# Expert loop of a two-block model: rows gathered already turned, biases in four row groups, four units of weights held, loads moved ahead

## The chip, the cores and the metric

The kernel runs on one core of a Trainium2 chip. The metric is the device time of one execution in microseconds; less is better. Three runs of the kernel before gave 2664.05, 2665.75 and 2666.48 us (median 2665.75). The profile is of one more execution.

## What is computed

A sequence of 256 tokens of width 1024 passes through two blocks, all in float32. The first block is two layers of a hybrid of convolution, retention and window attention. The second block is one layer: a token mixer with a bidirectional recurrence over 256 context and 256 latent tokens, and then a mixture of 32 experts of which each token takes 4. The change is in the last part and in what is loaded just ahead of it. Its reference, in short:

```
logits = h @ w_router + b_router                 # (256, 32)
top_val, top_idx = top_k(logits, 4); gates = softmax(top_val)
for each expert e, for the tokens that chose it:
    u   = h[tok] @ w1[e] + b1[e]                 # (n, 2048)
    glu = min(u[:, 0::2], 7); lin = clip(u[:, 1::2], -7, 7)
    act = glu * sigmoid(1.702 * glu) * (lin + 1)
    out[tok] += gate * (act @ w2[e] + b2[e])     # (n, 1024)
x = layer_norm(alpha * x + gt2 * out)
```

An expert has 8 MiB of w1 (1024 x 2048) and 4 MiB of w2 (1024 x 1024).

## The kernel before, in words

Each engine has its own program, and semaphores order them. The experts are done in jobs: one job is one expert with at most 64 of its tokens (SLOTS). There are 32 jobs, and one more for each further 64 tokens of an expert that has more; the count is computed on the chip (`turns`), and in the profiled execution it is 33. `moe_tensor`, `moe_scalar` and `moe_vector` each have a loop over the jobs; `moe_loads` is the loop of SyncE, which starts the transfers.

The weights of a job are six units of 2 MiB: units 0 to 3 are w1, units 4 and 5 are w2. There are six slots for them (`slots`: three of the ring that the whole kernel uses, and three of `ring2`). The load of unit j of job t+1 is started when TensorE has used unit j of job t (`e_unit`). Job 16 (`KEPT`) is special: its units 4 and 5 are loaded ahead of the loop into buffers of their own (`extra`), and in the loop only its units 0 to 3 are loaded.

TensorE does in a job, in this order (lines 2578 to 2631):

1. The biases of w1 for the job's expert: four products of a 32 x 64 selector with 32 x 512 of b1 (L2592), into banks 4 and 5. They all lie on partitions 0 to 31; two of them write the lower and two the upper 64 partitions of a bank.
2. The up projection: 32 products of 128 x 64 by 128 x 512 (L2601), stationary `hsel`, moving the weights.
3. The gather for the next job: four products with the stationary selector `sel` (128 x 64) and the moving tokens `h_tok` (128 x 512), into bank 6 (L2549).
4. The scatter of the job before: eight products of 64 x 128 by 64 x 256 into banks 0 to 3 (L2563), which hold the sums over all jobs.
5. Two transposes of the gated selector (L2614), four of the gathered rows (L2555, `turn_gathered`) and four of the job's hidden rows (L2621). The gathered and the hidden rows are read with a step of four elements (`[:, c::4]`).
6. The down projection: 16 products of 128 x 64 by 128 x 512 (L2629).

A float32 product is two pairs of LDWEIGHTS and MATMUL in the trace, a transpose is one. ScalarE copies between these steps: `gsel` (L2685, gathered rows out of bank 6), `selgT` (L2708), `hsel` (L2688), `hidT` (L2712) and `ye` (L2715), and computes the two sigmoids (L2703). VectorE makes the selectors and the gated product.

Ahead of the loop TensorE does the gather of job 0, starts the sums in banks 0 to 3 with b2 (L2539: eight products of 32 x 128 by 32 x 256, all on partitions 0 to 31, in two calls of `start_sums`), and turns the gathered rows between the two calls. SyncE starts job 0's unit 1 after the last weights of the token mixer, waits for the end of the mixer's output projection (`mo_done` 4), and then starts unit 2, unit 0, `grids`, `b2`, `b1`, units 3, 4, 5 and job 16's units 4 and 5.

Of the kernel before, what the change touches and what calls it, by code (L numbers as in the profile page):

```python
# [1332 lines left out]
def mixer_tensor(pe, nc, g):  # L1333
# [318 lines left out]
    for n in range(4):  # L1652
        pe.wait_ge(g["gn_squared"].sem, g["gn_squared"].at(None, n + 1))
        nc.tensor.matmul(flat[4 + n], blk64, g["squares"][:, n, :], start=True, stop=True).then_inc(
            g["gn_sum"].sem, g["gn_sum"].one())
# [43 lines left out]
def mixer_scalar(act, nc, g):  # L1699
# [188 lines left out]
    for n in range(4):  # L1888
        act.wait_ge(g["gn_sum"].sem, g["gn_sum"].at(None, n + 1))
        nc.scalar.activation(g["squares"][:, n, :], flat[n], ACT.Square).then_inc(g["gn_squared"].sem, g["gn_squared"].one())  # L1890
    for n in range(4):
        act.wait_ge(g["gn_sum"].sem, g["gn_sum"].at(None, 5 + n))
        nc.scalar.activation(g["squares"][:, n, :], flat[4 + n], ACT.Ln, bias=g["eps2"][:, 1:2], scale=1.0 / C2).then_inc(
            g["gn_log"].sem, g["gn_log"].one())
    act.wait_ge(g["gn_log"].sem, g["gn_log"].at(None, 4))
    for n in GN_ORDER:
        nc.scalar.activation(g["squares"][:, n, :], g["squares"][:, n, :], ACT.Exp, scale=-0.5).then_inc(
            g["gn_root"].sem, g["gn_root"].one())
# [12 lines left out]
def mixer_aliases(g):  # L1911

    g["norms"] = [g["squares"][:, NC:DN, 0:T], g["yy"][:, 0:NC, :]]
    g["cat"] = g["stack"][:, :, 0:T]

    g["incl"] = [g["squares"][:, 0:NC, :], g["stack"][:, NC:DN, :]]
    g["excl"] = [g["stack"][:, 0:NC, :], g["squares"][:, NC:DN, :]]
    g["gate"] = g["stack"][:, :, T:2 * T]
    g["bonus_in"] = g["m_k"].rearrange("p n (s t) -> p (n s) t", s=2)
    g["bonus"] = g["kd"][:, :, 0:T]  # L1920
    g["fa"] = g["iclr"][:, :, 0:T]
    g["spec"] = g["kk"][:, :, 0:T]
# [402 lines left out]
EXTRA = 16  # L2325
JOBS = N_EXPERTS + EXTRA
# [19 lines left out]
def moe_grids():  # L2346
# [3 lines left out]
    return np.concatenate([grids, np.arange(P)[:, None]], axis=1).astype(np.float32)  # L2350


def moe_signals(ctx, nc, g, hyb):
# [5 lines left out]
    for name, spent, base, per in (  # L2359
        ("u_first", "x_sum", 0, 1), ("ga_done", "conv_sum", 1, 1), ("gb_done", "ret_scores", 1, 1), ("st_done", "ret_o", 1, 1),  # L2360
        ("ht_done", "ret_var", 0, 1), ("ga_out", "x_root", 1, 1), ("st_out", "conv_root", 1, 1), ("ht_out", "decay_ready", 0, 1),
# [11 lines left out]
    g["extra_in"] = [follow(g["start_in"], g["start_in"].per, 1), Signal(ctx, nc, "extra_in", 1, 16)]  # L2373


def moe_memory(ctx, nc, g):
# [8 lines left out]
    sb("b2", [D], parts=N_EXPERTS)  # L2385
    sb("b1", [2 * D_FF], parts=N_EXPERTS)
    sb("grids", [2 * GRID + 1])
    sb("h3", [DC, T])
# [17 lines left out]
    sb("gT", [T], parts=N_EXPERTS)  # L2406
    sb("sel", [TC, SLOTS])
    sb("selg", [TC, 2, SLOTS])
    sb("bsel", [SLOTS])
    sb("selgT", [T])  # L2410
    sb("gsel", [4 * P])
    sb("hsel", [4, 2, SLOTS])
    sb("glu", [2, 2 * P])
    sb("lin", [2, 2 * P])
    sb("sig", [2, 2 * P])
    sb("hid", [4 * P])
    sb("hidT", [4, 2, SLOTS])
    sb("ye", [4 * P])
    sb("finrow", [2, T])
    sb("tiles", [T])  # L2420
    extra = sb("extra", [2, DC * UNIT])
    g["extra"] = {4: extra[:, 0], 5: extra[:, 1]}
    g["fin"] = g["h3"]

# [7 lines left out]
def moe_loads(sp, nc, g):  # L2432
    def unit(e, j, slot):

        if j < 4:
            rows = g["w1"][0, bass.ds(e, 1), (j // 2) * 4 * P:(j // 2 + 1) * 4 * P, :]
            src = rows.rearrange("o (p c) n -> p (o c) n", c=4)[:, 2 * (j % 2):2 * (j % 2) + 2, :]
            return sp.dma_start(slot.rearrange("p (c n) -> p c n", c=2), src)
        rows = g["w2"][0, bass.ds(e, 1), (j - 4) * 4 * P:(j - 3) * 4 * P, :]
        return sp.dma_start(slot.rearrange("p (c n) -> p c n", c=4), rows.rearrange("o (p c) n -> p (o c) n", c=4))  # L2440
# [12 lines left out]
    for j, s in zip((4, 5), g["extra_in"]):  # L2453
        unit(KEPT, j, g["extra"][j]).then_inc(s.sem, s.one())
# [3 lines left out]
    def job(t, units):  # L2458
        e = KEPT if type(t) is int else sp.value_load(g["jobs"][0:1, bass.ds(t, 1)], min_val=0, max_val=N_EXPERTS - 1)
        for j in units:  # L2460

            sp.wait_ge(g["e_unit"].sem, t * E_UNITS + (j + 1))
            unit(e, j, g["slots"][j]).then_inc(landed(j).sem, landed(j).unit)
# [3 lines left out]
    job(KEPT, range(4))  # L2467
# [19 lines left out]
MOE_LOOP = ("e_unit", "u_first", "ga_done", "st_done", "gb_done", "ht_done")  # L2487


def moe_tensor(pe, nc, g):  # L2490
# [87 lines left out]
    def job(t, kept=0):  # L2578
        def landed(j):
            if type(t) is int and j in g["extra"]:  # L2580
                s = g["extra_in"][j - 4]
                pe.wait_ge(s.sem, s.at(None, 1))
# [33 lines left out]
        pe.wait_ge(g["ga_out"].sem, g["ga_out"].at(t, 1))  # L2616
        turn_gathered().then_inc(g["gb_done"].sem, g["gb_done"].one())
# [41 lines left out]
def moe_scalar(act, nc, g):  # L2659
# [9 lines left out]
    nc.scalar.activation(g["finrow"][0:1, 0, 0:1], g["eps3"][0:1, 0:1], ACT.Exp)  # L2669
# [11 lines left out]
    nc.scalar.activation(g["gT"][:, :], flat[7][0:N_EXPERTS, 0:T], ACT.Copy).then_inc(  # L2681
        g["gates_out"].sem, g["gates_out"].one())

    def take_gathered():
        return nc.scalar.activation(g["gsel"][:, :], flat[6], ACT.Copy)  # L2685
# [5 lines left out]
    take_gathered().then_inc(g["ga_out"].sem, 1)  # L2691
    act.wait_ge(g["gb_done"].sem, g["gb_done"].at(None, 0))
# [7 lines left out]
    with act.Fori(0, turns) as t:  # L2700
# [16 lines left out]
    nc.scalar.activation(g["finrow"][0:1, 0, 0:1], g["eps3"][0:1, 0:1], ACT.Copy).then_inc(g["all_out"].sem, 1)  # L2717
    nc.scalar.activation(g["finrow"][0:1, 1, 0:1], g["eps3"][0:1, 0:1], ACT.Sqrt)
# [14 lines left out]
def moe_vector(dve, nc, g):  # L2733
# [77 lines left out]
    v.tensor_copy(g["bhot"][:, 0:N_EXPERTS], g["c"]("ident")[:, 0:N_EXPERTS])  # L2811
# [13 lines left out]
    dve.wait_ge(g["late_in"].sem, g["late_in"].at(None, 3))  # L2825
# [91 lines left out]
def program(nc, w, out):  # L2917
    with ExitStack() as ctx:
# [44 lines left out]
        moe["late_in"] = Signal(ctx, nc, "late_in", 3, 16)  # L2963
# [9 lines left out]
        def _(sp):  # L2973
# [7 lines left out]
            moe_loads(sp, nc, moe)  # L2981
# [86 lines left out]
```

## Time and profile before

| | us |
|---|---|
| median of three runs | 2665.75 (2664.05 to 2666.48) |
| profiled execution, its own time | 2661.23 |
| its span | 2658.4 |
| mean granted TensorE clock | 0.994 of full |
| TensorE busy | 2544.8 (96%) |
| VectorE busy | 924.9 (35%) |
| ScalarE busy | 583.4 (22%) |
| moved by DMA | 636.13 MB, mean 239 GB/s |

The span runs from the first instruction to the last; 2.8 us of the execution's time lie around it. PE is TensorE's matmul, PEld its weight load, and the two overlap. DVE is VectorE, ACT ScalarE, POOL GpSimd and SP SyncE. The jobs fill the span from about 1689 us to 2639 us.

### The profile page before, as it was taken

How to read it: one execution, taken by the hardware profiler on the slowest of the kernel's cores; microseconds unless marked ns; L12 is line 12 of the kernel's file. 1: busy time of each engine (PE TensorE's matmuls, PEld its weight loads, DVE VectorE, ACT ScalarE, POOL GpSimd, SP SyncE). 2: the span in 40 equal slices, each digit the busy share in tenths (PEclk: the TensorE clock that was granted, in tenths of full speed). 3: DMA queues.
4: the chain of work that ended last, by engine and by line, in shares of the span. 5: the costliest groups of instructions: out<-in, count | busy, mean ns of one | idle time of the engine just before them, and what ended most of it. 6: DMA issues, size and time to landing. Idle time of an engine off the chain costs nothing.

```text
span 2658.4 us, 42182 instructions
## 1 busy us (share of the span) xinstructions
PE 2544.8 (96%) x18014; PEld 1673.4 (63%) x18014; DVE 924.9 (35%) x2004; ACT 583.4 (22%) x1168; POOL 149.5 (6%) x124
## 2 busy tenths in 40 slices
PE   8999999999999999999997889899999999999998
PEld 6867878888884887888886777433333333333333
DVE  1863363312277245323476653311111111111112
ACT  2100233301100123220135433311111111111112
POOL 0050000000032000000003220000000000000000
PEclk9999999999999999999999999999999999999999
DMA  7555232344455422336410002999999999999995
GB/s 262 198 182 198 100 122 98 124 158 159 175 204 176 173 95 96 127 128 214 162 64 4 4 4 108 420 428 428 428 428 429 428 428 427 429 428 428 429 427 251
DMA packets 135029, 636.13 MB, mean 239 GB/s; under 512 B 5120, under 2 KB 5392, under 8 KB 109136
## 3 DMA queue, kind: packets, MB, share of 16 engines
q1 hardware_dynamic: 133904, 629.78, 59.6%
q0 software_dynamic: 992, 4.37, 0.5%
q8 instruction: 109, 1.79, 0.3%
q14 instruction: 24, 0.20, 0.0%
HBM read 633.08 MB, written 1.05 MB: 239 GB/s over the span
## 4 chain that ended last, share of the span: by engine, by line
PE 94%; ACT 2%; DVE 2%; issue 1%; DMA 1%; SPq 0%; ACTq 0%; DVEq 0%
PE bank L268 26%; PE bank L2601 17%; PE bank L2629 9%; PE bank L459 6%; PE bank L1405 4%; PE bank L481 4%; PE bank L289 4%; PE bank L1356 4%; PE bank L2563 2%; PE bank L2592 2%; PE bank L2549 2%; PE bank L1664 1%; PE bank L357 1%; PE bank L2621 1%; ACT hidT L2712 1%
## 5 line engine op out<-in xcount | busy, mean ns | idle before, releaser
L268 PE MATMUL bank<-hT,ring 128*128 128x256 f32 x3136 | 689.8, 380 | 2.5 <-DMA ring<-in_w_in 1.4
L268 PEld LDWEIGHTS bank<-hT,ring 128*128 128x128 f32 x3136 | 592.8, 190 | 94.6 <-issue 13.3
L2601 PE MATMUL bank<-ring,hsel 128*64 128x512 f32 x2112 | 462.0, 595 | 0.0
L2601 PEld LDWEIGHTS bank<-ring,hsel 128*64 128x64 f32 x2112 | 149.0, 137 | 310.8 <-issue 310.5
L2874 DVE TENSOR_SCALAR glu<-bank 128x256 f32<-128x256 f32 x66 | 28.0, 425 | 754.2 <-PE bank L2601 750.9
L2629 PE MATMUL bank<-ring,hidT 128*64 128x512 f32 x1024 | 226.8, 595 | 22.0 <-ACT hidT L2712 22.0
L754 DVE SCALAR_TENSOR_TENSOR a_buf<-v_pad,par,a_buf 128x256 f32<-128x256 f32 x480 | 215.8, 529 | 0.0
L2629 PEld LDWEIGHTS bank<-ring,hidT 128*64 128x64 f32 x1024 | 70.5, 137 | 156.2 <-issue 128.1
L1405 PE MATMUL bank<-ring 64*64 64x64 f32 (+1 forms) x5696 | 133.3, 229 | 25.6 <-issue 9.3
L1405 PEld LDWEIGHTS bank<-ring 64*64 64x64 f32 x5696 | 120.9, 137 | 40.6 <-issue 12.1
L2703 ACT ACTIVATE sig<-glu 128x256 f32<-128x256 f32 x66 | 27.5, 417 | 458.8 <-DVE glu L2874 458.8
L289 PE MATMUL bank<-ring,hT 128*128 128x512 f32 x256 | 111.4, 594 | 0.0
L481 PE MATMUL bank<-ro,ring 128*128 128x256 f32 x512 | 111.4, 379 | 0.0
L481 PEld LDWEIGHTS bank<-ro,ring 128*128 128x128 f32 x512 | 97.0, 190 | 13.8 <-issue 0.8
L1356 PE MATMUL bank<-stack,ring 128*128 128x256 f32 x480 | 104.5, 379 | 0.0
L1356 PEld LDWEIGHTS bank<-stack,ring 128*128 128x128 f32 x480 | 91.1, 190 | 12.7 <-issue 0.3
L289 PEld LDWEIGHTS bank<-ring,hT 128*128 128x128 f32 x256 | 48.2, 190 | 60.0 <-issue 60.0
L1232 POOL TENSOR_TENSOR ring<-ring,mcons 128x256 f32<-128x256 f32 x80 | 62.4, 815 | 250.9 <-DVE ring L2173 250.9
L2715 ACT ACTIVATE ye<-bank 128x512 f32<-128x512 f32 x33 | 19.7, 597 | 237.2 <-PE bank L2629 237.2
L2563 PEld LDWEIGHTS bank<-selgT,ye 64*128 64x128 f32 x544 | 49.7, 186 | 33.0 <-issue 26.8
L2563 PE MATMUL bank<-selgT,ye 64*128 64x256 f32 x544 | 67.9, 389 | 0.8 <-ACT finrow L2717 0.8
L2549 PE MATMUL bank<-h_tok,sel 128*64 128x512 f32 x272 | 64.2, 592 | 0.5 <-DVE sel L2796 0.5
(435 smaller groups left out, 2467.6 us busy)
## 6 DMA issues: line engine op xcount, KB each, us to landing
ring<-in_w SPq DMA_DIRECT2D x196, 2048.0 KB, 16.7
ring<-in_w_in SPq DMA_DIRECT2D x66, 2048.0 KB, 7.8
ring<-in_w_ada SPq DMA_DIRECT2D x12, 2048.0 KB, 8.0
ring<-in_w_ret_out SPq DMA_DIRECT2D x8, 2048.0 KB, 7.8
ring<-in_w_out SPq DMA_DIRECT2D x6, 2048.0 KB, 8.6
ring<-in_w_conv_out SPq DMA_DIRECT2D x4, 2048.0 KB, 8.3
ring<-in_w_attn_out SPq DMA_DIRECT2D x4, 2048.0 KB, 8.0
extra<-in_w SPq DMA_DIRECT2D x2, 2048.0 KB, 34.7
```

Source lines behind the costliest of these rows:

```text
L268: mm = nc.tensor.matmul(out[:, j, :], w[:, k, col + j * P:col + (j + 1) * P], rhs[:, k, :], start=(k == 0), stop=(k == DC - 1))
L289: mm = nc.tensor.matmul(out[:, :, :].rearrange("p a b -> p (a b)"), g["hT"][:, k, t * P:(t + 1) * P], w[:, k, :], start=(k == 0), stop=(k ...
L459: mm = nc.tensor.matmul(out[:, j, :], ws[k // DC][:, k % DC, cols + j * P:cols + (j + 1) * P], rhs[:, k, :], start=(k == 0), stop=(k == n ...
L481: mm = nc.tensor.matmul(out[:, j, :], w[:, k, col:col + P], g["ro"][:, row * DC + k, :], start=(row == 0 and j == 0 and k == 0), stop=(row ...
L754: ins = nc.vector.scalar_tensor_tensor(out=y[:, c, :], in0=v[:, c, t:t + T], scalar=w, in1=y[:, c, :], op0=ALU.mult, op1=ALU.add)
L1232: nc.gpsimd.tensor_tensor(g["cut"][:, k, d * NC:(d + 1) * NC, :], g["MP"][:, d * NC:(d + 1) * NC, :], row(mask[:, k, d, :], NC), ALU.mult) ...
L1356: mm = nc.tensor.matmul(flat[(q + 3) % 4][:, 0:T], w[:, k, j * P:(j + 1) * P], g["stack"][:, k, lo:lo + T], start=(k == 0), stop=(k == DC ...
L1405: mm = nc.tensor.matmul(out[at:at + 64], lhsT[lo:lo + 64], rhs[lo:lo + 64], start=start, stop=stop, skip_group_check=not (start and stop))
L2549: mm = nc.tensor.matmul(half(flat[6], side), g["sel"][:, t, :], g["h_tok"][:, t, side * UNIT:(side + 1) * UNIT], start=(t == 0), stop=(t = ...
L2563: mm = nc.tensor.matmul(g["bank"][b][:, at, :], half(g["ye"], side)[:, n * P:(n + 1) * P], half(g["selgT"], side), start=False, stop=last, ...
L2601: mm = nc.tensor.matmul(half(flat[4 + b], side), g["hsel"][:, 2 * (j % 2) + k, j // 2, :], w[:, at:at + UNIT], start=False, stop=(j == 3 a ...
L2629: mm = nc.tensor.matmul(half(flat[7], side), g["hidT"][:, c, j, :], w[:, at:at + UNIT], start=(j == 0 and c == 0), stop=(j == 1 and c == 3))
```

## The change

What it does:

- **Gather.** The operands change places: `h_tok` (128 x 128, read with a step of four elements) is stationary and `sel` (128 x 64) moves. The result lands in bank 6 in the layout of `hsel`, and one copy of ScalarE takes it there. The turning of gathered rows (`turn_gathered`, `take_gathered`, `gsel`, the semaphores `ga_out` and `gb_done`) goes.
- **Biases.** b1 and b2 lie in four groups of 32 partitions, each with a quarter of the columns, loaded by eight transfers in place of two. The selector and the gates (`bsel`, `gT`) stand four times over, once in each group; the gates are turned by eight products in place of two transposes. Each of the four bias products, and each of the eight of `start_sums`, takes the partitions of its group.
- **Buffers.** `h3`, the three grids of the overflow plan, and `glu`, `lin`, `sig`, `hid` share one buffer; `hidT` and `finrow` lie over `grids`; the mixer's group norm uses `m_k` in place of `squares`. The room goes to two more held units: job 16's units 2 to 5 are held, and the loop loads its units 0 and 1.
- **Loads.** Job 0's and the held units start in another order, and most of them earlier: four behind the mixer's last weights, one when the mixer's rows are done (`cat_ready` 2), one when half of its output projection is done (`mo_done` 2).

The diff, cut to its core:

```diff
@@ moe_memory
-    g["extra"] = {4: extra[:, 0], 5: extra[:, 1]}
+    g["extra"] = {2: extra[:, 0], 3: extra[:, 1], 4: extra[:, 2], 5: extra[:, 3]}
+    g["h3"] = shared[:, :].rearrange("p (c t) -> p c t", c=DC)
+    for i, name in enumerate(("before", "onehot", "work")):
+        g[name] = shared[:, i * GRID:(i + 1) * GRID].rearrange("p (o e) -> p o e", o=EXTRA)
+    for i, name in enumerate(("glu", "lin", "sig", "hid")):
+        g[name] = shared[:, i * 4 * P:(i + 1) * 4 * P]
...
@@ moe_loads
-    for j in (1, 2, 0):
-        if j == 2:
-            sp.wait_ge(g["mo_done"].sem, g["mo_done"].at(None, 4))
-        unit(0, j, g["slots"][j]).then_inc(landed(j).sem, landed(j).unit)
-    for dst, what in (("grids", g["grids_dram"]), ("b2", g["b2_dram"][0]), ("b1", g["b1_dram"][0])):
-        sp.dma_start(g[dst][:, :], what).then_inc(g["late_in"].sem, g["late_in"].one())
-    for j in (3, 4, 5):
-        unit(0, j, g["slots"][j]).then_inc(landed(j).sem, landed(j).unit)
-    for j, s in zip((4, 5), g["extra_in"]):
-        unit(KEPT, j, g["extra"][j]).then_inc(s.sem, s.one())
+    first(1)
+    kept(4)
+    first(4)
+    kept(3)
+    sp.wait_ge(mixer["cat_ready"].sem, mixer["cat_ready"].at(None, 2))
+    kept(5)
+    sp.wait_ge(g["mo_done"].sem, g["mo_done"].at(None, 2))
+    first(2)
+    sp.wait_ge(g["mo_done"].sem, g["mo_done"].at(None, 4))
+    first(0)
+    sp.dma_start(g["grids"][:, :], g["grids_dram"]).then_inc(g["late_in"].sem, g["late_in"].one())
+    for name, width in (("b2", D // GROUPS), ("b1", 2 * D_FF // GROUPS)):
+        for q in range(GROUPS):
+            sp.dma_start(g[name][q * N_EXPERTS:(q + 1) * N_EXPERTS, :],
+                         g[name + "_dram"][0, :, q * width:(q + 1) * width]).then_inc(g["late_in"].sem, g["late_in"].one())
+    first(3)
+    first(5)
+    sp.wait_ge(g["x_part"].sem, g["x_part"].at(None, DC))
+    kept(2)
...
-    job(KEPT, range(4))
+    job(KEPT, range(2))
@@ moe_tensor
-        mm = nc.tensor.transpose(flat[7][0:N_EXPERTS, t * P:(t + 1) * P], g["gate_map"][:, t, 0:N_EXPERTS], ident)
+        for q in range(GROUPS):
+            mm = nc.tensor.matmul(flat[7][q * N_EXPERTS:(q + 1) * N_EXPERTS, t * P:(t + 1) * P], g["gate_map"][:, t, 0:N_EXPERTS],
+                                  ident, start=True, stop=True)
...
-        for n in range(first, first + 4):
-            nc.tensor.matmul(g["bank"][n // 2][:, n % 2, :], g["b2"][:, n * P:(n + 1) * P], g["gT"][:, :],
-                             start=(n % 2 == 0), stop=False, skip_group_check=True)
+        for i in range(2):
+            for q in range(GROUPS):
+                lo, hi = q * N_EXPERTS, (q + 1) * N_EXPERTS
+                nc.tensor.matmul(g["bank"][q][:, i, :], g["b2"][lo:hi, i * P:(i + 1) * P], g["gT"][lo:hi, :],
+                                 start=(i == 0), stop=False, skip_group_check=True)
...
     def gather():
-        for t in range(TC):
-            for side in range(2):
-                mm = nc.tensor.matmul(half(flat[6], side), g["sel"][:, t, :], g["h_tok"][:, t, side * UNIT:(side + 1) * UNIT],
-                                      start=(t == 0), stop=(t == 1))
-        return mm
-
-    def turn_gathered():
         for c in range(4):
-            mm = nc.tensor.transpose(flat[6][:, c * P:(c + 1) * P], g["gsel"][:, c::4], ident)
+            for j in range(2):
+                for t in range(TC):
+                    mm = nc.tensor.matmul(flat[6][:, (2 * c + j) * SLOTS:(2 * c + j + 1) * SLOTS],
+                                          g["h_tok"][:, t, j * UNIT:(j + 1) * UNIT][:, c::4], g["sel"][:, t, :],
+                                          start=(t == 0), stop=(t == 1))
         return mm
...
+    pe.wait_ge(g["turned_out"].sem, g["turned_out"].at(None, 2))
     gather().then_inc(g["ga_done"].sem, 1)
-    start_sums(0)
-    pe.wait_ge(g["ga_out"].sem, g["ga_out"].at(None, 0))
-    turn_gathered().then_inc(g["gb_done"].sem, 1)
-    start_sums(4)
+    start_sums()
...
-                at = (2 * side + b) * UNIT
-                nc.tensor.matmul(half(flat[4 + b], side), g["bsel"][0:N_EXPERTS, :], g["b1"][:, at:at + UNIT], start=True, stop=False)
+                lo, hi = (2 * side + b) * N_EXPERTS, (2 * side + b + 1) * N_EXPERTS
+                nc.tensor.matmul(half(flat[4 + b], side), g["bsel"][lo:hi, :], g["b1"][lo:hi, :], start=True, stop=False)
...
-        pe.wait_ge(g["ga_out"].sem, g["ga_out"].at(t, 1))
-        turn_gathered().then_inc(g["gb_done"].sem, g["gb_done"].one())
@@ moe_scalar, in the loop
         act.wait_ge(g["ga_done"].sem, g["ga_done"].at(t, 1))
-        take_gathered().then_inc(g["ga_out"].sem, g["ga_out"].one())
+        take_rows().then_inc(g["gt_out"].sem, g["gt_out"].one())
         act.wait_ge(g["st_done"].sem, g["st_done"].at(t, 1))
         nc.scalar.activation(g["selgT"][:, :], flat[7][:, 0:T], ACT.Copy).then_inc(g["st_out"].sem, g["st_out"].one())
-        act.wait_ge(g["gb_done"].sem, g["gb_done"].at(t, 1))
-        take_rows().then_inc(g["gt_out"].sem, g["gt_out"].one())
@@ mixer: group norm
-        nc.scalar.activation(g["squares"][:, n, :], flat[n], ACT.Square).then_inc(g["gn_squared"].sem, g["gn_squared"].one())
+        nc.scalar.activation(g["gn_sq"][:, n, :], flat[n], ACT.Square).then_inc(g["gn_squared"].sem, g["gn_squared"].one())
...
```

## Rows read from the trace of the kernel before

**Rows 1.** The page: the chain that ended last, by engine.

```profile
PE 94%; ACT 2%; DVE 2%; issue 1%; DMA 1%; SPq 0%; ACTq 0%; DVEq 0%
```

**Rows 2.** The chain in order of time, one job and the next: start, us, what.

```profile
1733.58 1.72 PE bank L2549 x8
...
1739.50 7.09 PE bank L2629 x32
1746.59 1.86 PE bank L2592 x8
1748.45 13.88 PE bank L2601 x64
1762.33 1.72 PE bank L2549 x8
```

**Rows 3.** A stretch of the loop: length, busy of PE, PEld, DVE, ACT, POOL, clock, DMA, GB/s.

```profile
1704.23:2604.00 899.77, 877.79 (x4326) 329.70 (x4324) 126.69 (x384) 154.58 (x254) 0.00 (x0) 1.00 1.01 428
```

**Rows 4.** Landing of units 4 and 5 early; then of units 0 to 3, last job.

```profile
DMA to landing us min/median/max: 9.8/10.5/11.2
...
L2438 SPq DMA_DIRECT2D ring<-in_w x4: 332/332/342, 2586.2 to 2596.5; - x4
...
DMA to landing us min/median/max: 19.9/22.1/24.3
```

**Rows 5.** Timeline inside one job: start, us, engine, line, operation, shapes, idle before.

```profile
1704.65 1.88 PE L2549 MATMUL bank<-h_tok,sel 128*64 128x512 f32 x8
...
1706.47 2.00 PE L2563 MATMUL bank<-selgT,ye 64*128 64x256 f32 x16
...
1708.87 0.38 ACT L2708 ACTIVATE selgT<-bank 128x256 f32<-128x256 f32 x1 [1.69 <-PE bank L2614]
...
1709.30 0.56 PEld L2621 LDWEIGHTS bank<-shared_cons,hid 128*128 128x128 f32 x4 [0.18 <-ACT selgT L2708]
...
1710.09 0.60 ACT L2712 ACTIVATE hidT<-bank 128x512 f32<-128x512 f32 x1
```

**Rows 6.** Loads of 128 columns with little to move: timeline, then min/median/max in ns.

```profile
1679.00 0.39 PE L2523 MATMUL bank<-chosen_map,moec 128*128 128x32 f32 x2
1679.22 0.61 PE L2525 MATMUL bank<-chosen_map,shared_cons 128*128 128x32 f32 x4
...
1708.39 0.20 PEld L2614 LDWEIGHTS bank<-shared_cons,selg 128*128 128x128 f32 x2 [0.33 <-issue]
1708.56 0.56 PEld L2555 LDWEIGHTS bank<-shared_cons,gsel 128*128 128x128 f32 x4
...
L2614 PEld LDWEIGHTS bank<-shared_cons,selg x66: 138/140/143, 1708.4 to 2628.7; 128*128 128x128 f32 x66
L2555 PEld LDWEIGHTS bank<-shared_cons,gsel x136: 195/210/218, 1684.8 to 2629.1; 128*128 128x128 f32 x136
```

**Rows 7.** Lines by form: products that share the array in four tiles.

```profile
L232 PE MATMUL bank<-ring,cond 128*32 128x512 f32 x192 | 23.1, 598 | 0.0
L1405 PE MATMUL bank<-ring 64*64 64x64 f32 x5184 | 118.3, 223 | 25.2 <-issue 9.3 <-ACT ring L1833 5.1 <-DVE ring L2231 5.0
```

**Rows 8.** Timeline ahead of the loop; the last row is job 0's up projection.

```profile
1680.97 1.94 PE L2549 MATMUL bank<-h_tok,sel 128*64 128x512 f32 x8 [0.51 <-DVE sel L2796]
1682.84 1.99 PE L2539 MATMUL bank<-gT,b 32*128 32x256 f32 x8
...
1689.36 15.46 PE L2601 MATMUL bank<-ring,hsel 128*64 128x512 f32 x64
```

**Rows 9.** SyncE's issues; two stretches (columns as rows 3); landing of the held units.

```profile
1621.89 37.29 SPq L2438 DMA_DIRECT2D ring<-in_w  x3
...
1694.71 10.62 SPq L2438 DMA_DIRECT2D ring<-in_w  x4
...
1645.00:1650.00 5.00, 5.00 (x25) 4.40 (x24) 1.14 (x3) 0.00 (x0) 0.00 (x0) 1.00 0.00 0
1690.00:1695.00 5.00, 5.00 (x20) 1.56 (x18) 2.88 (x8) 0.61 (x1) 0.00 (x0) 0.76 0.99 419
...
extra<-in_w SPq DMA_DIRECT2D x2, 2048.0 KB, 34.7
```

More of the change, by code:

```diff
@@ L1653, in mixer_tensor @@
         pe.wait_ge(g["gn_squared"].sem, g["gn_squared"].at(None, n + 1))
-        nc.tensor.matmul(flat[4 + n], blk64, g["squares"][:, n, :], start=True, stop=True).then_inc(
+        nc.tensor.matmul(flat[4 + n], blk64, g["gn_sq"][:, n, :], start=True, stop=True).then_inc(
             g["gn_sum"].sem, g["gn_sum"].one())
@@ L2325 @@
 EXTRA = 16
+GROUPS = P // N_EXPERTS
 JOBS = N_EXPERTS + EXTRA
@@ L2349, in moe_grids @@
     grids = np.broadcast_to(np.concatenate([o.reshape(-1), e.reshape(-1)]), (P, 2 * GRID))
-    return np.concatenate([grids, np.arange(P)[:, None]], axis=1).astype(np.float32)
+    return np.concatenate([grids, np.arange(P)[:, None] % N_EXPERTS], axis=1).astype(np.float32)
 def moe_signals(ctx, nc, g, hyb):
@@ L2372, in moe_signals @@
         g[name] = follow(hyb[spent], DEPTH * hyb[spent].per + base, per)
-    g["extra_in"] = [follow(g["start_in"], g["start_in"].per, 1), Signal(ctx, nc, "extra_in", 1, 16)]
+    g["extra_in"] = Signal(ctx, nc, "extra_in", 4, 16)
 def moe_memory(ctx, nc, g):
@@ L2384, in moe_memory @@
     g["ec"] = lambda name: g["moec"][:, MOE_CONST[name][0]:MOE_CONST[name][1]]
[L2385 to L2388, printed above, removed]
-    sb("h_tok", [TC, D])
+    sb("selgT", [T])
+    sb("ye", [4 * P])
+    sb("b2", [D // GROUPS])
+    sb("b1", [2 * D_FF // GROUPS])
+    shared = sb("early_late", [8 * T])
+    sb("h_tok", [TC, D])
+    sb("gT", [T])
+    sb("selg", [TC, 2, SLOTS])
+    sb("bsel", [SLOTS])
+    sb("top", [TC, 8])
+    sb("few", [TC, 4])
+    sb("gap", [8])
+    extra = sb("extra", [4, DC * UNIT])
+    turned = sb("grids_late", [2 * GRID + 1])
     for name in ("logit", "above", "equal", "count", "chosen_map", "odds"):
@@ L2405, in moe_memory @@
     sb("jobs", [JOBS], mybir.dt.int32)
-    sb("gT", [T], parts=N_EXPERTS)
     sb("sel", [TC, SLOTS])
[L2408 to L2411, printed above, removed]
     sb("hsel", [4, 2, SLOTS])
[L2413 to L2419, printed above, removed]
-    sb("tiles", [T])
-    extra = sb("extra", [2, DC * UNIT])
-    g["extra"] = {4: extra[:, 0], 5: extra[:, 1]}
+    sb("tiles", [T])
+    sb("spot", [3])
+    g["extra"] = {2: extra[:, 0], 3: extra[:, 1], 4: extra[:, 2], 5: extra[:, 3]}
[4 more added lines that the diff above has]
+        g[name] = shared[:, i * 4 * P:(i + 1) * 4 * P]
+        if name != "hid":
+            g[name] = g[name].rearrange("p (b f) -> p b f", b=2)
     g["fin"] = g["h3"]
+    g["grids"] = turned
+    g["hidT"] = turned[:, 0:4 * P].rearrange("p (c h s) -> p c h s", c=4, h=2)
+    g["finrow"] = turned[:, 4 * P:8 * P].rearrange("p (a t) -> p a t", a=2)
 def moe_turns(eng, g):
@@ L2429, in moe_turns, with moe_unit @@
     return eng.value_load(g["turns"][0:1, 0:1], min_val=N_EXPERTS, max_val=JOBS - 1)
[L2432 to L2440, printed above, removed]
+def moe_unit(sp, g, e, j, slot):
+    if j < 4:
+        rows = g["w1"][0, bass.ds(e, 1), (j // 2) * 4 * P:(j // 2 + 1) * 4 * P, :]
+        src = rows.rearrange("o (p c) n -> p (o c) n", c=4)[:, 2 * (j % 2):2 * (j % 2) + 2, :]
+        return sp.dma_start(slot.rearrange("p (c n) -> p c n", c=2), src)
+    rows = g["w2"][0, bass.ds(e, 1), (j - 4) * 4 * P:(j - 3) * 4 * P, :]
+    return sp.dma_start(slot.rearrange("p (c n) -> p c n", c=4), rows.rearrange("o (p c) n -> p (o c) n", c=4))
@@ L2442, in landed, with moe_loads @@
+def moe_loads(sp, nc, g, mixer):
     def landed(j):
         return g["e_landed"][j]
-    for j in (1, 2, 0):
-        if j == 2:
-            sp.wait_ge(g["mo_done"].sem, g["mo_done"].at(None, 4))
-        unit(0, j, g["slots"][j]).then_inc(landed(j).sem, landed(j).unit)
-    for dst, what in (("grids", g["grids_dram"]), ("b2", g["b2_dram"][0]), ("b1", g["b1_dram"][0])):
-        sp.dma_start(g[dst][:, :], what).then_inc(g["late_in"].sem, g["late_in"].one())
-    for j in (3, 4, 5):
-        unit(0, j, g["slots"][j]).then_inc(landed(j).sem, landed(j).unit)
@@ L2453, in moe_loads, with first, kept @@
-    for j, s in zip((4, 5), g["extra_in"]):
-        unit(KEPT, j, g["extra"][j]).then_inc(s.sem, s.one())
+    def first(j):
+        moe_unit(sp, g, 0, j, g["slots"][j]).then_inc(landed(j).sem, landed(j).unit)
+    def kept(j):
+        moe_unit(sp, g, KEPT, j, g["extra"][j]).then_inc(g["extra_in"].sem, g["extra_in"].one())
+    first(1)
[5 more added lines that the diff above has]
+    sp.wait_ge(g["mo_done"].sem, g["mo_done"].at(None, 2))
@@ L2462, in job @@
             sp.wait_ge(g["e_unit"].sem, t * E_UNITS + (j + 1))
-            unit(e, j, g["slots"][j]).then_inc(landed(j).sem, landed(j).unit)
+            moe_unit(sp, g, e, j, g["slots"][j]).then_inc(landed(j).sem, landed(j).unit)
     with sp.Fori(1, KEPT) as t:
         job(t, range(E_UNITS))
-    job(KEPT, range(4))
+    job(KEPT, range(2))
     with sp.Fori(KEPT + 1, turns) as t:
@@ L2680, in moe_scalar @@
     act.wait_ge(g["gates_turned"].sem, g["gates_turned"].at(None, 1))
-    nc.scalar.activation(g["gT"][:, :], flat[7][0:N_EXPERTS, 0:T], ACT.Copy).then_inc(
+    nc.scalar.activation(g["gT"][:, :], flat[7][:, 0:T], ACT.Copy).then_inc(
         g["gates_out"].sem, g["gates_out"].one())
-    def take_gathered():
-        return nc.scalar.activation(g["gsel"][:, :], flat[6], ACT.Copy)
     def take_rows():
@@ L2980, in _ @@
             mixer_loads(sp, nc, mix)
[L2981 removed]
+            moe_loads(sp, nc, moe, mix)
             for i in range(4):
```

44 lines of the change are left out of this document (18 added, 26 removed).

## The prediction

> **What bounds the kernel now.** I read the chain of waits first: TensorE carries 94% of it [rows 1]. The change touches the experts' part, so I followed the chain there in order of time. It is TensorE in every job: gather 1.72 us, then 4.20 of scatter, transposes and waits up to 1739.50, down 7.09, bias 1.86, up 13.88. From one gather to the next is 1762.33 - 1733.58 = 28.75 us, and all 33 jobs repeat it [rows 2]. Then the stretch of the loop: DMA is busy throughout at 428 GB/s and the clock is 1.00 [rows 3]. A job's six units are 12.58 MB, so 29.4 us at that rate, more than TensorE's 28.75. The transfers fall behind by 0.6 us a job: early in the loop a unit lands some 10.5 us after its issue, in the last job 20 to 24 us after [rows 4]. The last unit 3 is issued at 2596.5 and lands 24.3 us later, at 2620.8 [rows 4]; it is needed after three quarters of the last up projection. 30 jobs after the one in rows 2 that starts at 1748.45 + 30 x 28.75 = 2611.1, so unit 3 is needed at 2621.5. TensorE therefore sets the end, with the transfers 0.7 us short of doing so. A job that gets shorter runs into the transfers unless these are relieved; one that gets longer by over 0.6 us leaves them behind.
>
> **Gather.** Removed: four products, eight pairs of load and matmul, 1.72 us on the chain [rows 2]. Added: 16 products, so 32 pairs, each with a 128 x 128 load and 64 moving columns. Two such pairs with only 32 moving columns, without a step, take 1679.22 - 1679.00 = 0.22 us, 0.11 each [rows 6]; two tiles with 512 columns take 1.72/8 = 0.215 a pair. With so little to move, the load sets the pace. The new loads also read with a step of four. Transposes show what that costs: a contiguous load of 128 columns follows the one before after 0.20 - 0.14 = 0.06 us, one with the step after (0.56 - 0.21)/3 = 0.12 [rows 6]. A transpose's contiguous load is twice as fast as a product's, so the step may hide beneath the 0.11, or add its 0.06 (0.17), or double as it does there (0.24 for the product's two passes). I take 0.12, since the step's row has this very shape and step: 32 x 0.12 = 3.84 us. From two column tiles to another tiling there is a hand-over: gather to scatter is 1706.47 - 1704.65 = 1.82 us for 1.72 of pairs, 0.10 more [rows 5], and the new gather has one such hand-over more, at its start. Together 3.94 - 1.72 = +2.22 us a job; +1.9 at 0.11, +3.8 at 0.17, +6.1 at 0.24.
>
> For this row the Trainium skill has a rule: "SBUF — State Buffer", section on the DMA port swizzle, says that SBUF has lines of 16 bytes, that an access which goes to a new line each time pays, and that two hits on a line absorb it. A step of four float32 is a new line for each element, and the load of 210 against 140 ns [rows 6] agrees. If a product's load reads each element twice in a row, the rule gives the 0.11; if it goes over the whole row twice, 0.24.
>
> **The turning that goes.** Four transposes, about 0.5 us. They lie between the selector's transposes and the moment that `selgT` is out: the loads of the two selector transposes start at 1708.39 [rows 6], ScalarE's copy runs 1708.87 to 1709.25, and the hidden rows' loads start at 1709.30 with that copy as the releaser [rows 5]. Without the turning TensorE waits there instead. On ScalarE `gsel` and `hsel` become one copy ahead of `selgT`; the gather that it waits for ends 1.9 us of scatter earlier than the selector's transposes, so `selgT` is not late. `hidT` starts at 1710.09 [rows 5] behind the hidden rows' transposes. Bounds 0 and -0.5 us; I take 0.
>
> **Biases.** Four products, eight pairs, 1.72 us and a hand-over [rows 2], on two column tiles. With four row groups all four can run side by side. No row has four row groups. But two column tiles take 13.88/64 = 0.217 us a pair of 512 columns [rows 2] and four take 23.1/192 = 0.12, and 64 x 64 tiles in all four quarters take 118.3/5184 = 0.023 us a pair of 64 columns, less than an eighth of 0.217 [rows 7]. So half the time, 0.86 us in place of 1.72: -0.86, bounds 0 and -0.86. The Trainium skill ("TensorE: Matmul & The Clock Gate", section on the speedup against the span model) gives 3.07 times for four row tiles; by that, as an estimate from the page, the four products take 1.12 us and the whole is 9 us longer.
>
> **Per job**: +2.22 - 0.86 = +1.36 us, thus 30.1; 33 jobs, +44.9 us.
>
> **Ahead of the loop.** The gather of job 0 starts at 1680.97 and the up projection at 1689.36 [rows 8]. After: gather 3.9, `start_sums` in four groups 0.9 (its first eight pairs took 1.99 in a row; now 16 four abreast) and a hand-over, bias 0.86 and a hand-over, so up at 1686.9: -2.5 us. The copy to `hsel` lies beside `start_sums`. The gates' eight products come before `sel` is there. If the groups don't run together it is +1 instead. Job 0's up takes 15.46 us against 13.88 in the loop, with the clock at 0.76 in part of it [rows 8, 9]; I leave that.
>
> **Held units and earlier loads.** Two units less in the loop are 2 x 4.9 us of transfer. DMA is idle at 1645 to 1650 and SyncE stands most of 37 us in its wait [rows 9], so the moved loads find room; six DMAs more cost SyncE under 0.5 us each. Behind its new waits (`cat_ready` 2, `mo_done` 2, `x_part`) stand only loads for the first up projection and later, and last a held one. The mixer's output weights are issued ahead of all of them. Worth 0 here, since TensorE bounds with 30.1 against 29.4 us a job. Were a job to stay at 28.75, it would be worth 0 too, by the 0.7 us in hand.
>
> **Sum**: 2658.4 + 44.9 - 2.5 = 2700.8 of span, 2703.6 of time against the profiled 2661.2. The runs' median stands 4.5 above that execution, so 2708 for the runs.
>
> **Rivals.**
> - *The step costs more.* At 0.17 us a load: 32 x 0.05 x 33 = +53, 2761. At 0.24: +127, 2835. For it: loads with a step take twice the pace in the only rows that have them. Against: a product's contiguous load is already at half the pace of a transpose's, which may cover it.
> - *The four groups don't run together*: the change does not do what it says. +0.86 x 33 + 3.5 = +32, 2740. For: no row has four row groups. Against: tiles of other kinds do overlap [rows 7].
> - *The clock falls in the gather*, where the array moves little for 3.9 us. Job 0's up is 1.6 us longer for it [rows 2, 8, 9]; once a job that is +53, 2761. Against: the clock is 1.00 through the loop's present waits [rows 3].
> - *Faster.* If the loads follow each other at 0.06 us, as contiguous transposes' do [rows 6], the gather is 2.02 us and a job 28.75 + 0.30 - 0.86 = 28.19, below the 29.4 of transfer. TensorE then offers 23 us, and the held units decide how much is used: the last landing comes 9.8 us earlier for them, and about 5 for the early start (the held ones landed in the median 34.7 us after issue, some 3 us behind the loop's first issue [rows 9]). With 0.7 in hand some 15 us: 2651. It decides from a gather below 2.6 us on. Against: 0.11 in rows 6, even without a step.
>
> **Chances.** Forecast 62% (2690 to 2725: loads of 0.11 to 0.13, and less overlap of the groups). Groups apart 8%. Load of 0.17 or a falling clock 10%. Load of 0.24 10%. Faster 7%; 3% that things cancel. The range 2688 to 2770 takes in the first three, 80%. No change means within 0.2%, 5.3 us, about what this measurement can tell. Faster 7%, same 3%, slower 90%.
>
> **What would show it.** The gather: 32 pairs, 3.6 to 3.9 us of chain a job against 1.72. Bias 0.95 to 1.0 against 1.86. From the selector's transposes to the hidden rows' loads still 0.9 us, half of it idle now. A job of 29.8 to 30.1 us; DMA in the loop below its full share, at 29.4/30.1, with landings that don't grow. Wrong if the gather's piece is under 2.6 us, or TensorE waits for a unit.

## The result, and the profile after

The changed kernel takes 2911.0 us (median of 4 runs, 2910.1 to 2912.1) against 2664.9 (4 runs of the kernel before, 2660.6 to 2666.5): the ratio is 1.0927, 95% interval 1.0908 to 1.0945. It is 246 us slower. Forecast were 2708 us and a range of 2688 to 2770: the sign was right, the size was not, and the range missed the time by 141 us. The profiled execution took 2910.1 us, span 2908.2.

The page of the changed kernel: span, busy engines, the granted clock in 40 slices, and the chain by engine, which stands against [rows 1].

```profile
span 2908.2 us, 43543 instructions
...
PE 2779.6 (96%) x18708; PEld 1923.8 (66%) x18708; DVE 927.5 (32%) x2004; ACT 563.7 (19%) x1134; POOL 149.6 (5%) x124
...
PEclk9999999999999999999999979989899898988888
...
PE 94%; ACT 3%; DVE 2%; issue 1%; DMA 1%; POOL 0%; SPq 0%; ACTq 0%; DVEq 0%
```

TensorE bounds as before. But the clock, which was 1.00 in the loop [rows 3], has fallen in most slices of it. The chain in order of time shows where (start, us, what), against [rows 2]. L2574 is the gather, L2584 the scatter, L2632 and L2637 the selector's and the hidden rows' transposes, L2645 down, L2610 the biases, L2619 up.

```profile
1707.39 7.66 PE bank L2574 x32
1715.05 3.72 PE bank L2584 x16
...
1721.67 9.92 PE bank L2645 x32
1731.60 1.02 PE bank L2610 x8
1732.61 13.88 PE bank L2619 x64
1746.50 7.66 PE bank L2574 x32
1754.16 3.72 PE bank L2584 x16
...
1760.30 7.09 PE bank L2645 x32
1767.38 1.02 PE bank L2610 x8
1768.40 13.88 PE bank L2619 x64
```

Three things are to be seen. The gather takes 7.66 us where 1.72 stood and about 3.9 was forecast. The biases take 1.02 for 1.86, as forecast. And work that the change doesn't touch is longer: the scatter 3.72 for 1.93 us, and in the first of these jobs the down projection 9.92 for 7.09.

Five-microsecond windows over the first of these gathers, and the whole loop from its first gather to its last (columns as rows 3), say why: the clock goes from full speed to its lower level (0.50 is 1.2 of 2.4 GHz) while the gather runs, and what follows pays.

```profile
1705.00:1710.00 5.00, 5.00 (x24) 3.26 (x20) 3.04 (x8) 0.84 (x2) 0.00 (x0) 1.00 1.00 426
1710.00:1715.00 5.00, 5.00 (x24) 4.88 (x23) 0.00 (x0) 0.00 (x0) 0.00 (x0) 0.54 1.00 429
1715.00:1720.00 5.00, 4.53 (x20) 2.96 (x20) 0.88 (x4) 0.98 (x2) 0.00 (x0) 0.50 0.72 306
1720.00:1725.00 5.00, 4.31 (x12) 1.59 (x14) 0.14 (x1) 0.60 (x1) 0.00 (x0) 0.50 0.00 0
...
1707.39:2867.80 1160.41, 1123.24 (x5057) 574.11 (x5057) 129.86 (x384) 137.43 (x225) 0.00 (x0) 0.87 0.81 337
```

The last window holds 32 jobs, so one is 1160.41/32 = 36.26 us in the mean, 7.51 more than before. Two terms of it are read off the chain: the gather +5.94 (7.66 - 1.72), the biases -0.84. What is left, 2.41 us a job, lies in work that the change doesn't touch, the scatter, the transposes and the down projection, at the slower clock. In the job that starts at 1707.39 the scatter is longer by 1.79, the two groups of transposes by 0.25 and 0.39 and the down projection by 2.83, together 5.26; in the next job it is 1.94 in all. The whole difference of the spans is 249.8 us: 2.6 up to the first gather of the loop (1707.39 against 1704.82, both in the chain), 240.2 in the 32 jobs, and 7.0 after the last gather's start (40.4 us to the end against 33.4: once more the gather and some clock).

### The profile page after: what moved, and what is told of

It reads as the page before. It is cut to its first block, busy times and chain, and to the rows that moved or that the text cites. A ratio compares the mean times of both kernels' runs of the same rounds, so it can differ in the third digit from the quotient of the medians.

```text
span 2908.2 us, 43543 instructions
## 1 busy us (share of the span) xinstructions
PE 2779.6 (96%) x18708; PEld 1923.8 (66%) x18708; DVE 927.5 (32%) x2004; ACT 563.7 (19%) x1134; POOL 149.6 (5%) x124
## 4 chain that ended last, share of the span: by engine, by line
PE 94%; ACT 3%; DVE 2%; issue 1%; DMA 1%; POOL 0%; SPq 0%; ACTq 0%; DVEq 0%
PE bank L268 23%; PE bank L2619 16%; PE bank L2574 9%; PE bank L2645 9%; PE bank L459 6%; PE bank L2584 4%; PE bank L1405 4%; PE bank L481 4%; PE bank L289 4%; PE bank L1356 4%; PE bank L2610 1%; PE bank L1664 1%; PE bank L2637 1%; PE bank L357 1%; ACT grids_late L2721 1%
## 5 line engine op out<-in xcount | busy, mean ns | idle before, releaser
L2619 PE MATMUL bank<-ring,hsel 128*64 128x512 f32 x2080 | 453.6, 594 | 0.0
L2619 PEld LDWEIGHTS bank<-ring,hsel 128*64 128x64 f32 x2080 | 146.5, 137 | 305.5 <-issue 305.5
L2574 PEld LDWEIGHTS bank<-sel,h_tok 128*128 128x128 f32 x1088 | 256.4, 328 | 27.3 <-issue 26.8
L2883 DVE TENSOR_SCALAR early_late<-bank 128x256 f32<-128x256 f32 x66 | 28.0, 425 | 750.4 <-PE bank L2619 747.0
L2645 PE MATMUL bank<-ring,grids_late 128*64 128x512 f32 x1024 | 245.7, 636 | 22.0 <-ACT grids_late L2721 22.0
L2574 PE MATMUL bank<-sel,h_tok 128*128 128x64 f32 x1088 | 262.8, 420 | 0.3 <-DVE sel L2805 0.3
L2645 PEld LDWEIGHTS bank<-ring,grids_late 128*64 128x64 f32 x1024 | 75.0, 146 | 172.0 <-issue 142.4
L2584 PE MATMUL bank<-selgT,ye 64*128 64x256 f32 x544 | 120.8, 617 | 0.8 <-ACT spot L2726 0.8
L2714 ACT ACTIVATE early_late<-early_late 128x256 f32<-128x256 f32 x66 | 27.6, 418 | 430.1 <-DVE early_late L2883 430.1
L2584 PEld LDWEIGHTS bank<-selgT,ye 64*128 64x128 f32 x544 | 83.5, 317 | 22.4 <-ACT spot L2726 1.7
```

What stands on the lines that cost most here:

```text
L2574: mm = nc.tensor.matmul(flat[6][:, (2 * c + j) * SLOTS:(2 * c + j + 1) * SLOTS], g["h_tok"][:, t, j * UNIT:(j + 1) * UNIT][:, c::4], g["se ...
L2584: mm = nc.tensor.matmul(g["bank"][b][:, at, :], half(g["ye"], side)[:, n * P:(n + 1) * P], half(g["selgT"], side), start=False, stop=last, ...
L2619: mm = nc.tensor.matmul(half(flat[4 + b], side), g["hsel"][:, 2 * (j % 2) + k, j // 2, :], w[:, at:at + UNIT], start=False, stop=(j == 3 a ...
L2645: mm = nc.tensor.matmul(half(flat[7], side), g["hidT"][:, c, j, :], w[:, at:at + UNIT], start=(j == 0 and c == 0), stop=(j == 1 and c == 3))
```

## The experiments

Seven kernels follow. Each is the changed kernel with one thing different, one of them with two. Two questions lead: is it the step of four in the loads that doubles the gather (or the 16 small products as such), and is the clock's fall a thing of its own? A third is what the other parts are worth once the gather is out of the way.

**The same gather from contiguous loads.** ScalarE's copies write the rows of `h_tok` in the order in which the gather reads them; the gather itself keeps its 16 products and their shapes, and nothing else changes.

```diff
-activation(g["h_tok"][:, t, b * UNIT:(b + 1) * UNIT], flat[2 * t + b], ACT.Copy)
+activation(g["h_tok"][:, t, b * UNIT:(b + 1) * UNIT].rearrange("p (c f) -> p c f", c=4),
+           flat[2 * t + b].rearrange("p (f c) -> p c f", c=4), ACT.Copy)
-    g["h_tok"][:, t, j * UNIT:(j + 1) * UNIT][:, c::4], g["sel"][:, t, :],
+    g["h_tok"][:, t, j * UNIT + c * P:j * UNIT + (c + 1) * P], g["sel"][:, t, :],
```

> The changed kernel, but ScalarE's copies write h_tok in the order that the gather reads, so that each of its 32 loads is contiguous. My theory (a product's load with a step of four goes at 0.233 us where a contiguous one goes at 0.111, and the long gather lets the clock fall): gather 3.6 us a job instead of 7.66, and with half the lull the clock holds; a job is 28.75 + 1.95 - 0.86 = 29.8 us, time 2695 to 2705. If the clock falls here too, 2730 to 2780. Rival (the pace of 0.233 comes from something else in the new gather: its moving side of 64 columns, the place of the buffers, the tiling): gather still 7.6 us, time about 2911.

Measured: 2701.4 us, ratio 1.0143 (1.0116 to 1.0170). Its chain for one job:

```profile
1795.83 3.72 PE bank L2574 x32
1799.54 1.93 PE bank L2584 x16
...
1825.73 3.71 PE bank L2574 x32
```

Its loop from first to last gather (columns as rows 3), and then the loads of its gather (min/median/max ns). The fence behind has the same loads in the changed kernel.

```profile
1706.11:2663.12 957.01, 919.91 (x5057) 409.31 (x5057) 129.84 (x384) 137.29 (x225) 0.00 (x0) 1.00 0.98 408
...
L2574 PEld LDWEIGHTS bank<-sel,h_tok x1088: 186/192/338, 1681.5 to 2666.5; 128*128 128x128 f32 x182
```

```profile
L2574 PEld LDWEIGHTS bank<-sel,h_tok x1088: 307/329/332, 1681.9 to 2874.9; 128*128 128x128 f32 x182
```

The gather halves to 3.72 us, a job is 29.90, the clock stays at 1.00 in the loop and the scatter is back at 1.93. The gather's +2.00 and the biases' -0.84 on 28.75 give 29.91, so nothing is left over for a clock. So the step, and not the number or size of the products, makes the load dear. This kernel is all but the one that the prediction described: 2701 measured, 2708 forecast.

One gather of this kernel does run at the slower clock: that of job 0, ahead of the loop, takes 6.43 us, with the granted clock at 0.50 from 1683.7 on. There a load without a step takes 333 ns, against 192 in the loop, while the stepped loads of the changed kernel take 329 ns at either clock.

**A step of two.** The loads read other columns, at a step of two elements; the gathered rows are so not those of the reference.

```diff
-    g["h_tok"][:, t, j * UNIT:(j + 1) * UNIT][:, c::4], g["sel"][:, t, :],
+    g["h_tok"][:, t, j * UNIT:(j + 1) * UNIT][:, (c // 2) * 2 * P + c % 2:(c // 2 + 1) * 2 * P:2], g["sel"][:, t, :],
```

> The changed kernel, but the gather's loads read every second element of a 256-wide piece in place of every fourth of 512, so it gathers other columns of the tokens and the numbers are not the reference's; the count and shapes of instructions are the same. Theory A (each element that lies on a line of 16 bytes of its own costs a second access, two on one line do not): the load goes at 0.11 to 0.12 us, gather 3.6 to 3.9 us a job, time about 2700. Theory B (any step costs, or the cost grows in proportion to the bytes stepped over): 0.17 to 0.233 us, time 2770 to 2911.

Measured: 2710.6 us (2 runs), ratio 1.0169 (1.0140 to 1.0198). Its gather in the chain, and its loads:

```profile
1770.04 3.91 PE bank L2574 x32
...
L2574 PEld LDWEIGHTS bank<-sel,h_tok x1088: 193/196/332, 1685.2 to 2676.8; 128*128 128x128 f32 x182
```

A pair of load and matmul comes every 3.71/32 = 0.116 us without a step, every 0.122 at a step of two, every 0.239 at four, the hand-overs at the ends of the gather included. The price is not proportional to the step: two is almost free, four doubles. That is what the rule on 16-byte lines gives ("SBUF — State Buffer" in the Trainium skill, section on the DMA port swizzle: two accesses that hit one line absorb it). At a step of two each line still holds two of the elements read, at four only one. The runs agree with it, with 3.91 and 7.66 us. The same passage of the Trainium skill gives four float32 as how far one can stride for free; these loads pay double at a step of four, and the measurement decides. That the line is the reason, and not another property of the step of four, isn't shown: steps of three and of eight weren't tried.

**The stepped gather in quarters**, one behind each of the four units of the up projection. Work and loads are the same; only the place differs, and with it the number of changes between the gather's shapes and those of the up projection.

```diff
             mm.then_inc(g["e_unit"].sem, g["e_unit"].one())
+            if j == 0:
+                pe.wait_ge(g["sel_ready"].sem, g["sel_ready"].at(t, 1))
+            mm = gather_part(j)
-        pe.wait_ge(g["sel_ready"].sem, g["sel_ready"].at(t, 1))
-        gather().then_inc(g["ga_done"].sem, g["ga_done"].one())
+        mm.then_inc(g["ga_done"].sem, g["ga_done"].one())
```

> The changed kernel with its stepped gather cut in four, one quarter behind each unit of the up projection, same work and same result. My theory (the clock falls because the gather keeps the array nearly idle for 7.66 us on end): quarters of 1.9 us don't let it fall; scatter back at 1.9 us, a job 28.75 + 5.9 - 0.86 + 0.6 for six more hand-overs = 34.4 us, time about 2850 (2835 to 2870). Rival (the clock falls for the loads' share of the time as such, however they lie): still 36 us a job, 2911 or more with the hand-overs.

Measured: 2858.6 us, ratio 1.0726 (1.0702 to 1.0750). Its chain at the end of one up projection, and its loop (columns as rows 3):

```profile
1782.06 2.01 PE bank L2578 x8
1784.07 1.93 PE bank L2588 x16
...
1707.00:2805.00 1098.00, 1060.90 (x5008) 526.46 (x5008) 126.89 (x384) 137.28 (x224) 0.00 (x0) 1.00 0.86 354
```

The quarters are 8.04 us a job, 0.38 more than in one piece, and the up projection has 0.44 more for the hand-overs between the tilings; still it is 52 us faster, since the clock no longer falls and the scatter takes 1.93. A job is 28.75 - 1.72 + 8.04 + 0.44 - 0.84 = 34.67 us, and 1799.96 - 1765.28 = 34.68 is seen. So the load's price stays (the kernel is still 194 us slower than the one before), and the fall of the clock is a second cost on top, of at least 52 us; by the sum above it is 32 x 2.41 = 77 us.

**In halves**, behind the second and the fourth unit: between the piece that lets the clock fall and the one that doesn't.

```diff
-            mm = gather_part(j)
+            if j % 2:
+                gather_part(j - 1)
+                mm = gather_part(j)
```

> As the kernel with the gather spread over the up projection, but in two halves of about 3.9 us, behind units 1 and 3, in place of four quarters. If the clock needs the whole 7.66 us of slow loads to fall, or nearly so, halves keep it up too: a job is 28.75 + 6.1 + 0.15 - 0.86 = 34.1 us, time about 2841, some 18 below the quarters for four hand-overs less a job. If 3.9 us are already enough, the clock is below 0.98 and the time is above 2860, up to 2900.

Measured: 2861.4 us, ratio 1.0738 (1.0710 to 1.0766), at the low end of what was expected with a falling clock; the mean granted clock, 0.984, is not quite as low as the 0.98 named there. Two stretches of the loop, the first half of a job in the one and a whole job's end in the other:

```profile
1775.54:2321.04 545.50, 526.93 (x2530) 266.67 (x2529) 64.86 (x192) 68.65 (x112) 0.00 (x0) 1.00 0.85 354
2321.04:2505.95 184.91, 179.10 (x791) 87.81 (x791) 20.28 (x60) 21.45 (x35) 0.00 (x0) 0.91 0.83 340
...
1775.54 3.88 PE bank L2578 x16
...
2357.88 3.93 PE bank L2578 x16
2361.80 8.44 PE bank L2623 x32
2370.24 3.88 PE bank L2578 x16
2374.11 2.95 PE bank L2588 x16
```

In 25 of the 32 jobs the clock holds, and a job is 545.50/16 = 34.09 us. In the rest, two at the start and the five from 2321.04 on, it falls, and the mean of these five is 184.91/5 = 36.98. The same program on the same work does both. Over the 32 jobs the falls cost 0.58 us a job in the mean, 19 us. What tips it in one job and not in the next isn't settled.

**Old gather and turning, the rest of the change kept** (biases in four groups, four held units, moved loads):

```diff
-        for c in range(4):
-            for j in range(2):
-                for t in range(TC):
-                    mm = nc.tensor.matmul(flat[6][:, (2 * c + j) * SLOTS:(2 * c + j + 1) * SLOTS],
-                                          g["h_tok"][:, t, j * UNIT:(j + 1) * UNIT][:, c::4], g["sel"][:, t, :],
-                                          start=(t == 0), stop=(t == 1))
+        for t in range(TC):
+            for side in range(2):
+                mm = nc.tensor.matmul(half(flat[6], side), g["sel"][:, t, :], g["h_tok"][:, t, side * UNIT:(side + 1) * UNIT],
+                                      start=(t == 0), stop=(t == 1))
...
+        turn_gathered(g["gsel"]).then_inc(g["gb_done"].sem, g["gb_done"].one())
```

> The changed kernel with the gather and the turning of before; biases in four groups, four held units and the earlier loads stay. My theory (all of the loss is the gather's loads and the clock that falls with them): TensorE needs 27.9 us a job, the transfers 29.4, so the transfers bind; they start without backlog and two units shorter: about 2650 (2643 to 2656), faster than before. Rival (some of the loss is from the shared buffers, the four groups or the moved loads): over 2665.

Measured: 2654.2 us (6 runs, 2650.3 to 2659.7), ratio 0.9954 (0.9939 to 0.9969). It is the fastest of all the kernels. The profiled execution is its slowest, 2659.7 us. One job of its chain; its loop (columns as rows 3); TensorE's waits for the ring of weights (us in all, times, the longest):

```profile
1764.31 1.72 PE bank L2574 x8
...
1777.31 1.02 PE bank L2616 x8
...
1792.21 1.72 PE bank L2574 x8
...
1764.31:2600.00 835.69, 798.19 (x4036) 297.62 (x4032) 118.23 (x358) 143.89 (x238) 0.00 (x0) 1.00 1.00 425
...
PEld bank L2625 <- DMA ring<-in_w: 43.4, 32, 2.1
PE bank L2625 <- DMA ring<-in_w: 18.7, 16, 1.2
```

TensorE needs 27.90 us a job, 0.85 less than before, which over 33 jobs would be 28 us. But 12.58 MB take 29.6 us at 425 GB/s, and the difference comes back as waits for weights: 10 of the 28 arrive at the end. Part of what the held units save is not used either. Once the two loads of job 16 are done, SyncE waits for TensorE to use unit 0 of that job before it starts the next load, though the slots of units 2 to 5 aren't needed for job 16: from 2152 to 2156 the queue moves at 8 GB/s.

**The same with the loads of before** (two held units, loads in the old order):

```diff
-    g["extra"] = {2: extra[:, 0], 3: extra[:, 1], 4: extra[:, 2], 5: extra[:, 3]}
+    g["extra"] = {4: extra[:, 2], 5: extra[:, 3]}
-        job(KEPT, range(2))
+        job(KEPT, range(4))
```

> As the kernel with the old gather and turning, but loads in the order of before and only units 4 and 5 of the held job (the two other buffers stay unused): of the change only the biases in four groups and the shared buffers are left. My theory: TensorE needs 27.9 us a job, but before had only 0.7 us in hand on the transfers, so nothing of the 0.86 a job arrives: 2660 to 2666, same as before; TensorE waits for units. Rival (TensorE is the bound, as the chain says, and the groups pay in full): 2665 - 28 - 3 = 2634.

Measured: 2662.1 us (10 runs), ratio 0.9987 (0.9977 to 0.9997): 2.4 us less than before, just clear of the noise. Its waits, in the same view:

```profile
PEld bank L2620 <- DMA ring<-in_w: 57.5, 42, 2.1
PE bank L2620 <- DMA ring<-in_w: 25.0, 21, 1.3
```

Without the two further held units and the early loads nearly all of the biases' gain is swallowed by transfers. The two together are thus worth 8 us (2662.1 against 2654.2), and only where TensorE's job is shorter than the transfers; what each is worth alone wasn't tried.

**The changed kernel with the loads of before**: the same edit of the loads, on the stepped gather.

> The changed kernel with its new gather and four-group biases, but the loads in the order of before and two held units instead of four. My theory: TensorE needs 36 us a job, far above the 29.4 of the transfers, so the loads don't matter: 2911, within 0.2%. Rival (the moved loads, or what they disturb ahead of the loop, cost part of the 246 us): under 2900.

Measured: 2912.9 us, ratio 1.0923 (1.0898 to 1.0949), against 1.0927 for the change. Its chain:

```profile
1746.34 7.66 PE bank L2569 x32
1754.00 3.72 PE bank L2579 x16
...
1760.63 9.79 PE bank L2640 x32
```

Gather, scatter and the longer down projection are all there with the old loads, so the held units and the moved loads play no part in the loss, nor in the clock's fall.

## Why the prediction was wrong

**The bound** was read rightly: TensorE sets the end before and after, with the transfers close behind. The two kernels with the old gather show how close.

**The gather** is the step that failed. The prediction put the load at 0.12 us and the 32 pairs at 3.84; they take 7.66, 0.239 a pair with the hand-overs. The working had the right row: a transpose's loads with a step of four come at 0.12 us, those without at 0.06, twice as often [rows 6]. It then took the absolute 0.12 of a transpose, although a product's load without a step already takes 0.11 to the transpose's 0.06. Read as a ratio the same row gives 2 x 0.11 = 0.22. The third of the bounds named there, 0.24, is what came, and it had got 10% and stood outside the range. The reason given with it, that a product goes over its row twice, no run shows. Measured against the forecast job, this is 33.85 - 30.11 = 3.74 us a job, 123 us in 33 jobs. Its rival alone was to give 2835.

**The clock** was a rival of its own, at +53 us and the worth of one longer job 0. It cost about 77 us. The two were priced as alternatives, and they aren't: in the loop the clock falls with the gather of twice the length. With contiguous loads (3.72 us in one piece) it stays at 1.00 there, with stepped loads in one piece it falls in all 32 (the shortest job is 34.98 us, and 33.85 would be one without a fall), in halves of 3.9 us in 7 of 32, in quarters of 2.0 in none. No case of the prediction had both; their sum, 2708 + 127 + 53 = 2888, would have come near. Against the profiled 2910.1, the 206.5 us by which the sum of 2703.6 was short are 123 for the load, 77 for the clock, 5 up to the first gather of the loop and 2 behind the last, less 1 that lies outside the span.

**The turning that goes** was put at 0, rightly. The timeline of the changed kernel, in the job of 1707.39, against [rows 5] (start, us, engine, what, idle before); the selector's transposes start at 1718.69:

```profile
1719.42 0.39 ACT L2719 ACTIVATE selgT<-bank 128x256 f32<-128x256 f32 x1 [3.74 <-PE bank L2632]
...
1719.86 1.13 PE L2637 MATMUL bank<-shared_cons,early_late 128*128 128x128 f32 x4 [0.47 <-ACT selgT L2719]
```

TensorE now stands for 0.47 us where it had turned rows, and starts the hidden rows when `selgT` is out, as it did before. At full clock, in the kernel with the contiguous gather, the chain has 0.84 us from the start of L2632 to that of L2637, against 0.85 before with the turning in between.

**The biases** came out at 1.02 us, hand-over included, against a forecast of 0.86 + 0.10; -0.84 for -0.86 a job. So the four groups run side by side, nearly without loss. The 3.07 times in the Trainium skill ("TensorE: Matmul & The Clock Gate", the section on the speedup against the span model) would have given 1.12 + 0.10 as an estimate; the run, with 1.02, is nearer to twice the old pace. The rival in which the groups don't overlap fell.

**Ahead of the loop** -2.5 us was forecast for the start of job 0's up projection; it starts at 1693.43, 4.1 later than before [rows 8]. The chain there:

```profile
1681.92 7.73 PE bank L2574 x32
1689.65 2.02 PE bank L2563 x16
1691.67 1.83 PE bank L2610 x8
1693.50 13.88 PE bank L2619 x64
```

The gather takes 3.8 us more than its 3.9. The granted clock is 0.50 from 1686 on, and at that clock the start of the sums (L2563) takes 2.02 us for the 0.9 forecast and the biases (L2610) 1.83 for 0.96. Some of this comes back: job 0's up projection takes 13.88 us, where it took 15.46 before at a lower clock, which the prediction had left.

The other 0.95 us had been lost ahead of the gather. About half is there before the mixer's output projection begins. The rest is this product, which starts at 1629.76 against 1628.75 before:

```profile
1629.76 4.55 PE L1664 MATMUL bank<-stack,ring 128*128 128x256 f32 x20 [1.23 <-DMA ring<-in_w_out]
```

It waits 1.23 us for the mixer's output weights, where 0.73 us of idle stood before, with ScalarE as the releaser. "Issued ahead of all of them" didn't protect this transfer. The same wait is in the traces of two more of the six kernels with the moved loads (those with the contiguous gather and with the old gather) and in none of the three with the old loads. So it goes with the moved loads, though not in every execution; that they take share of the DMA engines from the transfer is likely, not shown.

**Held units and earlier loads** at 0: right, by the changed kernel against itself with the old loads (1.0927 and 1.0923). The transfers' side answered as foretold: DMA at a share of 0.81 in the loop, and landings that don't grow (9.7 us in the median of the loop's 187 loads). But "worth 0 too" for a job of 28.75 doesn't carry further down: with 27.9 us a job they are worth 8.

**The rival on the other side** (a gather below 2.6 us, 2651 us) fell with the gather. Its mechanism, a TensorE job shorter than the transfers and the held units deciding how much of it counts, is what the kernel with the old gather shows, with 2654.2 us against 2662.1 without them.

## What to carry to other kernels

An operation that costs nothing to remove (four transposes beside a wait) can cost much to replace: where loads set the pace, a step of four in the stationary operand's rows doubled the price of each. Here one permuted write ahead of the loop gave the same order of the output at the pace of loads without a step, and the kernel still lost 1.4%, since 32 pairs at 0.116 us stand for 8 at 0.215. Take a slowdown from a row as a ratio and also as a difference, and let both stand in the range. And price rivals that feed each other together: here the longer gather, 7.66 us in one piece, also brought the clock down for the work behind it.

## What the runs showed of the hardware

- In gathers of 32 pairs, a product's float32 load of 128 columns and its matmul of 64 columns come every 0.116 us without a step, every 0.122 at a step of two elements, every 0.239 at four (hand-overs included).
- The stepped gather takes 7.66 us although the clock is halved for part of it, in all jobs alike, and its loads take 329 ns at either clock: at these two levels they don't go by TensorE's clock. Loads without a step do: 192 ns at 1.00, 333 at 0.50. So does the scatter: 3.72 us at 0.50, 1.93 at 1.00.
- TensorE is counted as busy all through the gather (5.00 of 5.00 us from 1710 to 1715) while its granted clock is at 0.54 in the mean.
- At full clock, eight pairs of 32-row tiles with 512 columns in four row and two column groups take 1.02 us with the hand-over, where two column tiles took 1.86.
